# First block of a hybrid decoder step: the norm by tile, eight table products behind the first rows, page table by GpSimd

## What is computed

```python
def _rms_norm(x, g):
    xf = x.astype(jnp.float32)
    y = xf * lax.rsqrt(jnp.mean(xf * xf, axis=-1, keepdims=True) + EPS)
    return (y * g.astype(jnp.float32)).astype(x.dtype)

def _mix_inputs(x, norm_attn, w_in):
    y = _rms_norm(x, norm_attn) @ w_in          # (rows, 1024) @ (1024, 2840)
...
    return jax.nn.gelu(xb @ w1) @ w2            # _compress, xb: (n, blocks, 2, 64 * 64)
...
    bias = bias_tab[_t5_bucket(rel)]            # 32 buckets, 16 heads, added to every logit
```

## Time and profile before

| | |
|---|---|
| median of 3 runs | 2256.63 us (2254.52 to 2258.96) |
| the profiled execution | 2255.5 us, its span 2253.5 us |
| TensorE busy | 2108.8 us, 94% of the span |
| VectorE, ScalarE, GpSimd busy | 1014.1, 519.7, 474.6 us |
| granted TensorE clock, mean | 0.968 |

### The profile page before, as it was taken

The page is one execution under the profiler, slowest core; times in us unless marked ns, Lnnn a source line. Parts: engine busy times, 40 slices in busy tenths (PEclk is TensorE's granted clock), DMA queues, the critical chain, the costliest instruction groups (busy, mean ns, idle before and its releaser), DMA issues. The chain is left out here.

```text
span 2253.5 us, 31733 instructions
## 1 busy us (share of the span) xinstructions
PE 2108.8 (94%) x12498; PEld 1374.5 (61%) x12498; DVE 1014.1 (45%) x2435; ACT 519.7 (23%) x1101; POOL 474.6 (21%) x667
## 2 busy tenths in 40 slices
PE   6989999997967885999999999999999999999998
PEld 3445466664635664666676446888888888544443
DVE  4044455402425543666676225667776765200110
ACT  3111101012213432776676111111111111000100
POOL 1434234102014650112222001223232222000000
PEclk9999999998788997999999999999999999999999
DMA  7467477643577996122251313665666332500200
GB/s 212 160 214 281 186 283 291 238 152 93 206 282 286 385 397 224 58 90 85 78 157 40 118 66 132 224 204 187 224 223 207 132 98 90 188 1 10 78 21 19
DMA packets 150649, 372.78 MB, mean 165 GB/s; under 512 B 36871, under 2 KB 89087, under 8 KB 132448
## 3 DMA queue, kind: packets, MB, share of 16 engines
q1 hardware_dynamic: 120678, 149.37, 21.0%
q0 software_dynamic: 25280, 149.44, 17.0%
q10 hardware_dynamic: 4544, 71.95, 9.0%
HBM read 343.42 MB, written 98.60 MB: 196 GB/s over the span
## 5 line engine op out<-in xcount | busy, mean ns | idle before, releaser
L2652 PE MATMUL ff_ps<-ff_hx,ff_aw 128*128 128x264 f32 x2464 | 550.1, 386 | 0.9 <-DVE ff_hx L2891 0.9
L2652 PEld LDWEIGHTS ff_ps<-ff_hx,ff_aw 128*128 128x128 f32 x2464 | 467.3, 190 | 80.8 <-issue 1.2
L730 DVE STREAM_TRANSPOSE sel_space<-sel_space 128x512 f32<-128x512 f32 x256 | 155.4, 674 | 165.6 <-PE in_psH L539 165.6
L503 PE MATMUL in_ps<-in_w,in_xT 128*128 128x512 f32 (+1 forms) x512 | 201.5, 547 | 0.0
L1113 DVE CUSTOM_DVE_ANT_0 pa_L<-pa_psS,pa_T 128x512 f32<-128x512 f32 (+3 forms) x288 | 138.9, 532 | 59.4 <-PE pa_psS L969 58.3
L1093 ACT ACTIVATE pa_L<-pa_L,pa_nm 128x640 f32<-128x640 f32 (+3 forms) x192 | 141.9, 741 | 45.1 <-DVE pa_nm L1123 43.2
L503 PEld LDWEIGHTS in_ps<-in_w,in_xT 128*128 128x128 f32 x512 | 95.0, 191 | 93.5 <-issue 87.6
L539 PE MATMUL in_psH<-sel_space 128*64 128x256 f32 (+1 forms) x1152 | 123.1, 369 | 11.2 <-DVE sel_space L721 11.2
L969 PE MATMUL pa_psS<-pa_kT,pa_qT 64*128 64x512 f32 (+3 forms) x576 | 114.9, 505 | 18.6 <-POOL pa_qT L1036 18.6
L628 ACT ACTIVATE in_yout<-in_ps 128x128 f32<-128x128 f32 (+5 forms) x88 | 41.3, 480 | 390.4 <-PE in_ps L503 213.4
L3013 DVE TENSOR_TENSOR ff_work<-ff_ps,ff_work 128x512 f32<-128x512 f32 (+1 forms) x18 | 12.3, 685 | 238.0 <-PE ff_ps L2730 139.3
(11 more groups left out here) (381 smaller groups left out, 2671.0 us busy)
## 6 DMA issues: line engine op xcount, KB each, us to landing
out_new_a_k_s<-in_cache_a_k ACTq DMA_DIRECT2D x8, 4088.0 KB
out_new_a_v_s<-in_cache_a_v ACTq DMA_DIRECT2D x8, 4088.0 KB
ff_aw<-in_w_up SPq DMA_DIRECT2D x44, 512.0 KB, 7.8
in_w<-in_w_in SPq DMA_DIRECT2D x5, 2048.0 KB, 18.7
sel_space<-in_cache_a_k SPq DMA_DIRECT2D x8, 1024.0 KB
sel_space<-in_cache_a_v SPq DMA_DIRECT2D x8, 1024.0 KB
ff_hx<-in_w_down SPq DMA_DIRECT2D x14, 512.0 KB, 4.7
sel_space<-in_cache_a_k SPq DMA_DIRECT2D x24, 256.0 KB
```

The costliest lines, as they stand in the source:

```text
L503: mm = pe.matmul(ps[0:n, b, 0:width], xT[:, k, t * P:t * P + n], w[:, at % WBUF, k, 0:width], start=(k == 0), stop=(k == KC - 1))
L730: last = dve.transpose(put[:, dh, :, k * HD:k * HD + HD].rearrange("p t (g b) -> p t g b", g=2), got[:, :, :, dh, :])
L2652: mm = pe.matmul(ps[:, bank_of(x, j, g), 0:H2], aw[:, j % 2, at, k, :], hx[:, bt, k, g * H2:g * H2 + H2], start=(k == 0), stop=(k == KH - 1))
```

## The change

Three edits of `front`:
- Of the 13 table products the first five stay in front. Behind them come all nine row tiles, then the chunks; one table product stands behind each of the eight prompt row tiles of the first chunk. NX is 23. `tab_op` has to live longer and moves from `yout` to columns 12288 and on of `pre.space`.
- Squares, mean, reciprocal, root and scaling are done tile by tile, with one tile's lead, and ScalarE and VectorE copy out the first five table products before the first square.
- `odd` and the page table (five small loads, four of them of single words) are issued by GpSimd at its start instead of by ScalarE.

```diff
-    shares = [chunks[0:5], chunks[5:9], chunks[9:13]]
-    jobs = []
-    for g in range(NG):
-        jobs += [("b", i, c) for i, c in shares[g]]
-        for t in range(3 * g, 3 * g + 3):
-            jobs += [("x", t, 0), ("x", t, 1)]
+    NB0 = 5
+    jobs = [("b", i, c) for i, c in chunks[0:NB0]]
+    for t in range(NTILE):
+        jobs += [("x", t, 0), ("x", t, 1)]
     NX = len(jobs)
+    tables_left = list(chunks[NB0:])
...
                 src, job = later.pop(0)
                 jobs.append((*job, src))
+            if tables_left and t < NTILE - 1:
+                jobs.append(("b", *tables_left.pop(0)))
...
-        tab_op = yout[0:35, :, :].rearrange("p a n -> p (a n)")[:, 0:AW]
+        tab_op = pre.space[0:35, 12288:12288 + AW]
...
-            def root(g):
-                act.wait_ge(s_ms, 2 * g + 2)
-                nc.scalar.activation(rstd[:, 3 * g:3 * g + 3], rms2[:, 3 * g:3 * g + 3], ACT.Sqrt).then_inc(s_rstd, 1)
+            def root(t):
+                act.wait_ge(s_ms, 2 * t + 2)
+                nc.scalar.activation(rstd[:, t:t + 1], rms2[:, t:t + 1], ACT.Sqrt).then_inc(s_rstd, 1)
...
             act.wait_ge(s_one, 1)
+            for j in range(NB0):
+                if on_act[j]:
+                    copy_out(act, j, copy).then_inc(s_ev[0], 1)
             squares(0)
+            squares(1)
             root(0)
-            squares(1)
-            before = -2
             for what, n in order:
-                if what == "job" and on_act[n]:
-                    if before < first_x[1] <= n:
-                        root(1)
-                        squares(2)
-                    if before < first_x[2] <= n:
-                        root(2)
-                    before = n
+                if what == "job" and on_act[n] and n >= NB0:
+                    if jobs[n][0] == "x":
+                        t = jobs[n][1]
+                        if t + 2 < NTILE:
+                            squares(t + 2)
+                        if t + 1 < NTILE:
+                            root(t + 1)
                     copy_out(act, n, copy).then_inc(s_ev[0], 1)
...
-            for j in (x for x in range(NX) if not on_act[x]):
-                for g in range(NG):
-                    if before < first_x[g] <= j:
-                        norm(g)
-                before = j
-                copy_out(dve, j, lambda o, i, s: dve.tensor_scalar(o, i, s, None, ALU.mult)).then_inc(s_ev[1], 1)
+            turned = lambda o, i, s: dve.tensor_scalar(o, i, s, None, ALU.mult)
+            for j in range(NB0):
+                if not on_act[j]:
+                    copy_out(dve, j, turned).then_inc(s_ev[1], 1)
+            norm(0)
+            for j in range(NB0, NX):
+                if not on_act[j]:
+                    if jobs[j][1] + 1 < NTILE:
+                        norm(jobs[j][1] + 1)
+                    copy_out(dve, j, turned).then_inc(s_ev[1], 1)
...
+            pool.dma_start(odd[:, :], io["c_odd"][:, :]).then_inc(s_pg, 16)
+            for d in range(2):
+                pool.dma_start(ptrc[d:32:2, :], bass.AP(io["page_table"].tensor, 0, [[1, 16], [16, 4 * NB], [1, 1]]),
+                              allow_slow_non_contiguous=True).then_inc(s_pg, 16)
```

More of the change, by code:

```diff
@@ L195, in front @@
     span_of = {ch: [j for j, x in enumerate(jobs) if x[0] in "nsq" and x[1] == ch] for ch in range(6)}
-    first_x = {g: min(j for j, x in enumerate(jobs) if x[0] == "x" and x[1] == 3 * g) for g in range(NG)}
     last_b = max(j for j, x in enumerate(jobs) if x[0] == "b")
@@ L618, in _, with squares @@
                           allow_slow_non_contiguous=True).then_inc(s_fb, 16)
[L619 to L625, removed]
             def copy(o, i, s):
                 return nc.scalar.activation(o, i, ACT.Copy, scale=s)
[L630 to L637, removed]
-            def root(g):
-                act.wait_ge(s_ms, 2 * g + 2)
-                nc.scalar.activation(rstd[:, 3 * g:3 * g + 3], rms2[:, 3 * g:3 * g + 3], ACT.Sqrt).then_inc(s_rstd, 1)
+            def squares(t):
+                if t % 3 == 0:
+                    act.wait_ge(s_x[t // 3], 48)
+                if t >= 2:
+                    act.wait_ge(s_sq, t - 1)
+                n = rows_of(t)
+                nc.scalar.activation(sq[t % 2][0:n, :], xin[0:n, t, :], ACT.Square,
+                                     accum_out=ss[0:n, t:t + 1]).then_inc(s_sq, 1)
+            def root(t):
+                act.wait_ge(s_ms, 2 * t + 2)
+                nc.scalar.activation(rstd[:, t:t + 1], rms2[:, t:t + 1], ACT.Sqrt).then_inc(s_rstd, 1)
             def half_copy(r):
@@ L683, in _, with norm @@
         def _(dve):
-            def norm(g):
-                c = slice(3 * g, 3 * g + 3)
-                dve.wait_ge(s_sq, 3 * g + 3)
+            def norm(t):
+                c = slice(t, t + 1)
+                n = rows_of(t)
+                dve.wait_ge(s_sq, t + 1)
                 dve.tensor_scalar(ms[:, c], ss[:, c], 1.0 / D, EPS, ALU.mult, ALU.add).then_inc(s_ms, 1)
-                dve.wait_ge(s_ms, 2 * g + 1)
+                dve.wait_ge(s_ms, 2 * t + 1)
                 dve.reciprocal(rms2[:, c], ms[:, c]).then_inc(s_ms, 1)
-                dve.wait_ge(s_rstd, g + 1)
-                if g == 0:
+                dve.wait_ge(s_rstd, t + 1)
+                if t == 0:
                     dve.wait_ge(s_gn, 16)
[L693 to L696, removed]
+                dve.scalar_tensor_tensor(out=xin[0:n, t, :], in0=xin[0:n, t, :], scalar=rstd[0:n, t:t + 1],
+                                         in1=gain[0:n, :], op0=ALU.mult, op1=ALU.mult).then_inc(s_xn, 1)
             def indices():
@@ L749, in _ @@
             dve.wait_ge(s_one, 1)
-            before = -1
-            for j in (x for x in range(NX) if not on_act[x]):
-                for g in range(NG):
-                    if before < first_x[g] <= j:
-                        norm(g)
-                before = j
-                copy_out(dve, j, lambda o, i, s: dve.tensor_scalar(o, i, s, None, ALU.mult)).then_inc(s_ev[1], 1)
+            turned = lambda o, i, s: dve.tensor_scalar(o, i, s, None, ALU.mult)
[8 more added lines that the diff above has]
+                    copy_out(dve, j, turned).then_inc(s_ev[1], 1)
             indices()
@@ L788, in _ @@
             pool.memset(w2, 0.0).then_inc(s_wz, 1)
+            pool.dma_start(odd[:, :], io["c_odd"][:, :]).then_inc(s_pg, 16)
+            for d in range(2):
+                pool.dma_start(ptrc[d:32:2, :], bass.AP(io["page_table"].tensor, 0, [[1, 16], [16, 4 * NB], [1, 1]]),
+                              allow_slow_non_contiguous=True).then_inc(s_pg, 16)
+            for d in range(2):
+                pool.dma_start(ptr[d:P:2, :], bass.AP(io["page_table"].tensor, 0, [[1, NPAGE], [NPAGE, NB], [1, 1]]),
+                              allow_slow_non_contiguous=True).then_inc(s_pg, 16)
             pool.wait_ge(s_pe, NX)
```

## The result

The changed kernel takes 2284.4 us (median of four, 2279.89 to 2296.39) against 2255.57 for the kernel before in the same session: ratio 1.0136, 95% interval 1.0101 to 1.0172. It is slower, by 28.8 us where 17.4 were forecast (the interval reaches from 22.8 to 38.8 us), and lies above the range, which ended at 2280.0. The profiled execution is the slowest of the four, 2296.39 us, with a span of 2294.5. Over the whole span TensorE's share of busy time hardly tells the two kernels apart, 93% against 94%.

A forecast was written before the change was run, and what follows sets the result against it. It took TensorE, full for most of the first block, as the bound. Opening -1.3, clock +1.7, seven products +6.3, hole +9.7, join +1.0 sum to +17.4; 2255.5 + 17.4 = 2272.9 us, range 2261.9 to 2280.0.

The forecast's parts named there:

- the hole: TensorE's wait in front of the compression, for stores and reloads of rows: from 11.2 to 21 us, term +9.7.
- the join: Joining the sample's partial sums (1.04 us) leaves the cover of the first compression step and is paid after it: +1.0.
- 8 x 2.65: Opening: eight more tiles at 2.65 us each after the first scaling, first weight product near 45.8 instead of 47.1: -1.3.
- +1 if the operands of the first product land a little later: High end of the opening's term, with the page table's small loads going out beside the first table product's operands.
- 3.4 us at half rate: Clock term: TensorE still at 1.2 GHz when the weight products begin, losing 1.7 us.
- 7 x 0.9 = 6.3: Seven table products between the first weight chunk's row tiles, where TensorE has no idle time, at 0.9 us each: +6.3.
- I take 9.2, for that gather is over by then: SyncE's 15 issues behind the last table product take 9.2 us instead of the 12.07 measured beside a large gather.
- The weights do not hinder the reloads: Rival: weights and reloads share the DMA engines without loss, +3.6 instead of +9.7, 2266.8 us; chance 0.16.
- The reloads are quick: Rival: reloads before the compression take 3.4 us instead of 10.9, total 2265.3 us; chance 0.08.
- The opening shrinks: Rival: operands 3 us earlier, VectorE's busy time as pace and a clock that is up, 2265.0 us; chance 0.07.
- The delay vanishes: Rival: TensorE's waits behind the first block (9.5 and 11.9 us) swallow its delay, 2255.5 us, not slower; chance 0.06.
- the change wins: Rival: the delay vanishes and the opening is short as well, about 2248 us; chance 0.03.

The follow-up runs named there:

- pages_act: The changed kernel with the page table's loads and `odd` back on ScalarE's queue; 2308.09 us against 2283.12 for the kernel before, ratio 1.0106.
- again: The changed kernel itself, unaltered, timed once more on another chip; 2307.24 us against 2283.12 for the kernel before, ratio 1.0102.
- fill_late: The kernel before with the compression's first step one job later and the third chunk's weights issued behind the reloads; 2264.44 us against 2277.57, ratio 0.9948.
- interleaved: The kernel before with the norm tile by tile and one table product behind each of the opening's first eight tiles; 2286.58 us against 2277.79, ratio 1.0036.
- late_weights: The kernel before with the third chunk's weights issued behind the eight reloads; 2274.59 us against 2277.57, ratio 0.9988.
- fill: The kernel before with the compression's first step one job later, behind one more row product; 2269.56 us against 2277.57, ratio 0.9965.

## Why the prediction was wrong, step by step

The sign and the mechanism held: 23.7 us of wait behind the stores of the tables, weights ahead of the reloads in one queue, a clock at 1.2 GHz where the weight products begin, nothing swallowed behind the block. The sizes were off, nearly all to one side. Of the 7.1 us by which the block's delay was missed, the hole has 2.8, the seven products 1.6, the opening 1.4, the clock 0.8 and the join 0.5.

- **"8 x 2.65", the opening at 45.8 (-1.3): it was +0.1.** The pace was 2.54, 0.9 less over eight tiles; the stretch from the last scaling to the first weight product was 3.0, 0.6 more. What failed is the other end, "+1 if the operands of the first product land a little later", which I had not put into the term: they landed 1.9 late, and `pages_act`, without the small loads beside them, had them at 8.7.
- **"3.4 us at half rate" (+1.7): +2.5.** The step itself took 3.64 instead of 1.92, as forecast; the rest is in the first row product, 7.93 us instead of 7.13. In `again` that one takes 7.13 and the term is +1.6, so this part of the miss is the run's.
- **"7 x 0.9 = 6.3": 7.9.** One product takes 1.03 between row products, not 0.90 as in a row of eight, and the pitch of a row tile went from 6.98 to 8.13, 1.15 each. Of these 1.15 the product's own pitch is 0.96; the key transpose in front of it and the row product behind it take some 0.1 more each. The row of eight was the wrong row for a product between others of another shape.
- **"I take 9.2, for that gather is over by then": 12.56, more even than the 12.07 taken as the high end.** This is the step that failed most, and its reason was wrong: the four far stores, priced at 4 x 0.49, took 5.71. In the kernel before they took 4.19, from 54.3 to 58.5, and the gather that was blamed moved its data in the main from 57 on (last two columns, DMA share and GB/s, of the kernel before):

```profile
54.00:56.00 2.00, 2.00 (x5) 0.57 (x3) 0.00 (x0) 0.00 (x0) 1.70 (x2) 1.00 0.78 82
...
58.00:60.00 2.00, 2.00 (x6) 0.90 (x5) 0.00 (x0) 0.00 (x0) 2.00 (x5) 1.00 1.05 359
```

  The `w2` loads, which did stand beside it, fell from 3.72 us to 2.44, where 2.64 was forecast. The place of the list in the changed kernel, beside GpSimd's stores of the last row tile:

```profile
120.00:126.00 6.00, 6.00 (x16) 2.56 (x14) 0.00 (x0) 0.20 (x2) 0.57 (x2) 1.00 0.83 122
```

  The DMA engines were busy 0.83 of the time there. The fourteen profiles tell the two causes apart in the main. Right behind the stores of all three tables (416 KB) the far stores take 4.19 to 5.24 us at the old place (seven profiles) and 5.70 to 5.78 at the new one (four); without a table just ahead 1.99, in each of three, with the gather being issued beside them. So the tables just ahead in the queue cost 2 to 3 us, and some 1 us more goes with the new place; no run moves one of the two by itself. Behind the list the forecast held: 16.93 us from the weights' issue to VectorE's start, 17.4 forecast.
- **The join (+1.0): 1.44.** It runs right behind a step at a granted clock of 0.50. The price of 1.04 was one at full clock.
- **The range.** Its high end gave the list and the opening room, but the products and the join, priced by one row each, had none, and the sum of the block's five terms came out at 24.5, exactly the range's edge (2280.0). The other 4.3 us of the median lie outside these terms, and inside the interval of the measurement.

The profiled execution, the slowest of the four, is 40.9 us above that of before: 24.5 in the first block, the rest in blocks that the change does not touch. The most of it is in `sample_selected`. From its first product of `L2080` (`L2084` with the change) to its last of all: 183 us in the profile of before, 193 in the profile of after, 208 in that of `again`, 207 in `fill_late`, the fastest kernel of its chip. TensorE's waits there, of the changed kernel on the first chip and then on the second:

```profile
PE sb_psT L2084 <- ACT sel_space L2228: 13.4, 8, 4.5
```

```profile
PE sb_psT L2084 <- ACT sel_space L2228: 19.1, 14, 3.8
```

The same code waits 5.7 us more on another chip, and the kernel before takes 2277 to 2283 us on three others instead of 2255.6. In the profile of after this wait is what it was in that of before (13.4 and 13.3); of the 10 us there 4.5 are two waits that before has not, and 5.7 are more busy time of TensorE at a lower granted clock (0.93 against 0.96). I can say that this block varies, not why.

**The rivals.** "The weights do not hinder the reloads" fell: 16.1 us right behind them, 10.5 ahead of them. "The reloads are quick" fell: 10.5 with nothing ahead. The fit of the Trainium skill (DMA: Bandwidth & Descriptors, Anatomy of one DMA) is given for one DMA issued by GpSimd, and 4.4 us for the 1 MB was an estimate from it; these are eight loads issued by SyncE, and no run comes near it. The rule of the Trainium skill (DMA: Bandwidth & Descriptors, Queues, rings and completion order), that an engine takes one queue's descriptors in ring order, agrees with the rates, 399 GB/s and then 123. "The opening shrinks" holds for the moved products alone (39.3) and was undone by the norm by tile, above all by the copies put ahead of the first square. "The delay vanishes" and "the change wins" found nothing: the waits behind the block stayed.

## What to carry to other kernels

Before moving work to a later place, look at who stores its result: an in-order queue that waits for the last of several results holds back everything listed behind that wait, and here it cost more than the moved work itself. Split such a list by what each entry needs, and put the transfers that a stalled engine waits for ahead of those that it needs later. And price a moved instruction by a row from the place where it will stand (its neighbours, its clock, its DMA traffic). Look, too, at what stands ahead of the first link of a chain: three copies put in front of the first square made every row of the opening some 4 us later, more than the finer steps behind it cost.

## What the runs showed of the hardware that was not expected

- In `interleaved` TensorE was busy for 13.00 of 13 us with 128-column transposes and 16-row products, and the profile gives a granted clock of 1.00, but each took nearly twice its shortest time: 1.97 for eight transposes, which take 1.07 at their fastest in the changed kernel, and 1.89 for a product of 1.03. That is the pace that other stretches show at a granted clock of 0.50, so here the durations tell the speed and the granted clock does not; why is open. The full pace is there with the first row product (7.23 us).
- With five small loads issued by GpSimd, four of them of single words, the first table product's operands land some 1 to 2 us later (9.9 to 10.85 us in the five profiles that have them there, 8.4 to 9.0 in the nine others).
- The same issue on SyncE costs 0.42 us or 2.00, by its place: `L421`'s four stores of the changed kernel had 422, 1577 and 2001 ns as shortest, median and longest.
- Identical openings differ: the first weight product of the kernel before's opening starts at 47.1, in `late_weights` at 48.6, in `fill` at 45.8, in `fill_late` at 46.3. One to two us at the block's end cannot be read from a single profile.
